# Shorter windows for the cached sequences, and the sampled rows' pass placed between the prompt's last units

## The reference, cut to what matters

```python
def finish(x, attn, pool, w_o, ...):
    mix = einsum(concat([attn, pool]), w_o)
    x1 = layer_norm(ALPHA * x + mix, ln1_g, ln1_b)
    hid = silu(x1 @ w_gate) * (x1 @ w_up)
    return layer_norm(ALPHA * x1 + hid @ w_down, ln2_g, ln2_b)

# prompt: q, k, v, logf, u = project(xp); attention over 1024 rows; pool_mix; finish
# sample, for each of 8 rows, with its own pages of the cache:
s = einsum(q, concat(cache_k[pages], k_new)) * 64 ** -0.5 + decay   # 8 heads, 4097 keys
out = einsum(softmax(s), concat(cache_v[pages], v_new))
# then finish() for the 8 rows, with the same weights (1024 x 2816 gate and up, 2816 x 1024 down)
```

## Time and profile before

| | us |
|---|---|
| median of 3 runs (1572.34 to 1581.2) | 1578.72 |
| profiled execution, own time | 1583.57 |
| its span, first to last instruction | 1581.6 |
| PE busy | 1397.7 (88%) |
| DVE busy | 719.6 (46%) |
| POOL busy | 551.9 (35%) |
| mean granted TensorE clock | 0.930 of full speed |

### The profile page before, as it was taken

How to read it: one execution, slowest core, us unless ns; L and a number is a source line. 1 busy time by engine, 2 the same in 40 slices (tenths; PEclk the granted TensorE clock), 3 DMA queues, 4 the chain that set the end, 5 groups by cost and what they waited for, 6 DMA issues and landing times.

```text
span 1581.6 us, 21048 instructions
## 1 busy us (share of the span) xinstructions
PE 1397.7 (88%) x7585; PEld 1110.2 (70%) x7585; DVE 719.6 (46%) x1000; ACT 361.4 (23%) x513; POOL 551.9 (35%) x211
## 2 busy tenths in 40 slices
PE   7998989999568458997999999999899999998875
PEld 5898989898468456775767767776677777766421
DVE  4745343445323283455444474635454634124702
ACT  4434444423100043211020112121102111111300
POOL 1010000031142335646555547375554572120500
PEclk9999999999778778998999999999999999999865
DMA  6321110100532304765667656686567665424895
GB/s 239 104 67 54 41 54 27 41 34 1 187 119 99 135 1 153 258 217 167 205 206 231 212 185 211 214 262 191 188 210 231 212 205 183 128 90 162 300 355 194
DMA packets 103031, 251.85 MB, mean 159 GB/s; under 512 B 12560, under 2 KB 13969, under 8 KB 97672
## 3 DMA queue, kind: packets, MB, share of 16 engines
q1 hardware_dynamic: 99632, 239.64, 45.5%
q0 software_dynamic: 3296, 10.88, 2.0%
HBM read 240.84 MB, written 9.86 MB: 159 GB/s over the span
## 4 chain that ended last, share of the span: by engine, by line
PE 73%; DVE 10%; DMA 7%; issue 3%; ACT 3%; SPq 3%; POOL 1%; DVEq 0%; ACTq 0%
PE PSM L1156 28%; PE PSM L1174 14%; PE PSM L959 10%; DMA AR<-ws 4%; PE PSM L1025 4%; PE PSM L1200 4%; PE PSM L1126 3%; PE PSM L972 3%; PE PSM L1011 2%; DMA WR<-w_o 1%; SPq L406 1%; SPq L401 1%; PE PSM L1271 1%; PE PSM L1258 1%; DVE PND L1609 1%
## 5 line engine op out<-in xcount | busy, mean ns | idle before, releaser
L627 POOL TENSOR_TENSOR AR<-AR,QB 128x2048 f32<-128x2048 f32 x64 | 298.6, 4671 | 162.7 <-DMA AR<-cache_k 162.5
L634 POOL TENSOR_TENSOR WL<-WR,WH 128x1024 fp32r<-128x1024 f32 x55 | 134.9, 2454 | 327.1 <-ACT WH L839 327.1
L1156 PE MATMUL PSM<-XH,WH 128*128 128x512 f32 x704 | 226.8, 403 | 0.0
L1156 PE MATMUL PSM<-XL,WH 128*128 128x512 f32 x704 | 221.9, 396 | 0.0
L1156 PE MATMUL PSM<-XH,WL 128*128 128x512 f32 x704 | 221.7, 396 | 0.0
L1531 DVE TENSOR_REDUCE SC<-AR 128x32 f32<-128x2048 f32 x64 | 145.8, 2278 | 101.8 <-POOL AR L627 101.8
L1646 DVE TENSOR_TENSOR ACC<-ACC,PSM 128x512 f32<-128x512 f32 x176 | 118.4, 684 | 136.4 <-PE PSM L1174 136.1
L1156 PEld LDWEIGHTS PSM<-XH,WH 128*128 128x128 f32 x704 | 129.0, 189 | 51.2 <-issue 23.5
L839 ACT CAST WH<-WR 128x1024 fp32r<-128x1024 f32 x55 | 57.6, 1048 | 469.3 <-PE PSM L1156 220.4
L1156 PEld LDWEIGHTS PSM<-XH,WL 128*128 128x128 f32 x704 | 133.1, 189 | 31.6
L1156 PEld LDWEIGHTS PSM<-XL,WH 128*128 128x128 f32 x704 | 133.0, 189 | 31.5
(11 more groups left out here) (233 smaller groups left out, 2121.6 us busy)
## 6 DMA issues: line engine op xcount, KB each, us to landing
AR<-cache_k SPq DMA_DIRECT2D x256, 256.0 KB, 3.3
AR<-cache_v SPq DMA_DIRECT2D x256, 256.0 KB, 3.4
AR<-ws SPq DMA_DIRECT2D x37, 1024.0 KB, 7.2
WR<-ffn SPq DMA_DIRECT2D x66, 512.0 KB, 4.6
WR<-w_in SPq DMA_DIRECT2D x16, 512.0 KB, 4.1
WR<-xT SPq DMA_DIRECT2D x8, 512.0 KB, 5.4
AR<-negF_d SPq DMA_DIRECT2D x8, 512.0 KB, 4.0
WR<-w_o SPq DMA_DIRECT2D x4, 1024.0 KB, 7.0
```

The source lines that it names most:

```text
L627: pool.tensor_tensor(keys, keys, QB[:].rearrange("p (o n) -> p o n", o=1).to_broadcast([P, CH, AW]), ALU.mult).then_inc(k_mul, 1)
L634: pool.tensor_tensor(lo, WR[:, e % WS, :], hi.bitcast(F32), ALU.subtract).then_inc(ffn_lo, 1)
L1156: ins = pe.matmul(out[:, hc], (hi, lo)[a][:, k * P:(k + 1) * P], x[b][:, k, hc], start=(k == 0 and n == 0), stop=(k == KC - 1 and n == 2))
```

## The change

The window of a cached sequence has 52 units instead of 62, so the 8 windows end at unit 416 and no longer at 496. The tables of units inside a window are drawn closer: the multiplications of keys stand 4 to 6 units apart and no longer 6 or 7, the values 11 or 12 units apart and no longer 15. The gap from the last values of a window to the first steps of the next stays as it was.

The sampled rows' pass is placed from unit 416 on. Its output product stands at 418 to 424, its first layer norm at 427 to 434, and the gate, up and down tiles at 438 to 521, some 2.5 units apart, so that all of it lies among the prompt's units. To free banks 0 and 1, which the prompt uses until its end, gate and up now share bank 7: a tile holds two chunks of gate and two of up, gate goes to column groups 0 and 1, up to 2 and 3. A full group has four such tiles GU, in place of two G and two U. One copy on ACT replaces the two copies of L895 and L1723, and the sum is made of four matmuls with a mask of 16 columns in place of eight with 8. The second layer norm of the 8 rows stands at units 523 to 525 of DVE's list. The layer norms' vectors g and b pass through one buffer, with a load between them (FACTORS1, OFFSETS1).

```diff
-WIN = 62
+WIN = 52
-VALUES = (9, 24, 39, 54)
+VALUES = (9, 21, 32, 44)
-OWN, COLUMNS, MAXIMUM, KEEP, HEADMAX = 57, 59, 60, 60, 61
-KMUL = (3, 10, 16, 23, 29, 36, 42, 49)
+OWN, COLUMNS, MAXIMUM, KEEP, HEADMAX = 47, 49, 50, 50, 51
+KMUL = (3, 8, 14, 19, 25, 30, 36, 40)
 KRED = tuple(o + 4 for o in KMUL)
 KLOAD = (0, 1) + tuple(o + 1 for o in KRED[:-2])
...
-        order += [(kind, g, r) for kind in "GU" for r in range(parts(g))]
-        order += [("D", g - 1, r) for r in range(parts(g - 1))] if g >= 1 else []
-        order += [("S", g, 0)]
...
+        order += [("GU", g, r) for r in range(parts("GU", g))]
+        order += [("D", g - 1, r) for r in range(parts("D", g - 1))] if g >= 1 else []
+    order += [("D", TGROUPS - 1, r) for r in range(parts("D", TGROUPS - 1))]
+    units = {step: TSTART + 5 * n // 2 + 3 * (n >= parts("GU", 0)) for n, step in enumerate(order)}
+    return units, [units["GU", g, parts("GU", g) - 1] + 2 for g in range(TGROUPS)]
...
-                if kind in "GU":
+                if kind == "GU":
...
-                            pe.wait_ge(silu_done, FT)
...
-                    rounds = ((r, 0),) if cols == HALF else ((0, 0), (1, 4 * cols))
-                    for k, at in rounds:
+                    elif r == 0:
+                        pe.wait_ge(e_hid, g)
+                    rounds, last = (1, 3) if cols == HALF else (2, 1)
+                    for a in range(rounds):
                         for q in range(4):
-                            ins = pe.matmul(PSM[32 * q:32 * q + 32, "GU".index(kind), 0:cols], CSP[:, 4 * k + q, :],
+                            k = 2 * (rounds * r + a) + q % 2
+                            ins = pe.matmul(PSM[32 * q:32 * q + 32, 7, 0:cols], CSP[:, k, :],
...
-                for kind, src in enumerate((gate_s, up_s)):
-                    for i in range(tiles):
-                        at = (4 * kind + i) * NB
-                        ins = pe.matmul(PSM[:, 7, at:at + NB], src[:, i * P:(i + 1) * P], blkmask[:], start=True, stop=True)
+                for i in range(min(4, FT - 4 * g)):
+                    ins = pe.matmul(PSM[:, 7, 2 * NB * i:2 * NB * (i + 1)], gu_s[:, i * P:(i + 1) * P], gumask[:],
+                                    start=True, stop=True)
...
-                dve.tensor_copy(up_s[:, 0:n], PSM[:, 1, 0:n]).then_inc(e_us, 1)
...
-            dve.wait_ge(t_used, len(STREAM))
-            sample_mean(2, e_var)
-            sample_scale(2)
+                if u == SAMPLE2:
+                    dve.wait_ge(t_used, len(STREAM))
+                    sample_mean(2, e_var)
+                if u == SAMPLE2 + 2:
+                    sample_scale(2)
```

More of the change, by code:

```diff
@@ L128, in sample_steps, with parts @@
 def sample_steps():
-    def parts(g):
-        return 2 if 4 * g + 4 <= FT else 1
     order = []
     for g in range(TGROUPS):
-        order += [(kind, g, r) for kind in "GU" for r in range(parts(g))]
-        order += [("D", g - 1, r) for r in range(parts(g - 1))] if g >= 1 else []
-        order += [("S", g, 0)]
[L138 to L144, removed]
+        order += [("GU", g, r) for r in range(parts("GU", g))]
[3 more added lines that the diff above has]
+    return units, [units["GU", g, parts("GU", g) - 1] + 2 for g in range(TGROUPS)]
+def parts(kind, g):
+    full = 4 * g + 4 <= FT
+    return {"GU": (2, 4), "D": (1, 2)}[kind][full]
+CSPAD = NB * WIN
+MIX, RESID, SQRT1, SCALE1, FACTORS1, OFFSETS1 = (CSPAD + n for n in (2, 11, 12, 13, 14, 18))
+TURN1, TURNED1, TSTART = (CSPAD + n for n in (20, 21, 22))
+STEPS_S, SUMS = sample_steps()
+STREAM = [("W", n, 0) for n in range(4)] + list(STEPS_S)
 TINDEX = {step: n for n, step in enumerate(STREAM)}
-SUNIT = {("W", n, 0): MIX + n for n in range(4)} | STEPS_S
+SUNIT = {("W", n, 0): MIX + 2 * n for n in range(4)} | STEPS_S
 NORM2 = BEGIN["D", NPAIR - 1] + 2
-LAST = max(SUNIT.values()) + 3
+SAMPLE2 = max(SUNIT.values()) + 2
+LNVEC2 = BEGIN["D", NPAIR - 1] - 4
+LAST = max(SAMPLE2 + 5, NORM2 + 2 * RT + 4)
 def weight_order():
@@ L886, in sample_root, with sample_partials @@
                 act.activation(sd[0:NB, RT, 0:1], sd[0:NB, RT, 1:2], ACT.Sqrt).then_inc(e_sd, 1)
-            def sample_gate(g):
+            def sample_partials(g):
                 n = min(HALF, DFF - g * HALF)
-                act.wait_ge(t_used, TINDEX["G", g, 0 if n < HALF else 1] + 1)
+                act.wait_ge(t_used, TINDEX["GU", g, parts("GU", g) - 1] + 1)
                 if g == 0:
-                    act.wait_ge(hl_done, FT)
+                    act.wait_ge(k_mul, NB * NCH)
                 else:
                     act.wait_ge(e_sum, g)
-                act.copy(gate_s[:, 0:n], PSM[:, 0, 0:n]).then_inc(e_gs, 1)
+                act.copy(gu_s[:, 0:n], PSM[:, 7, 0:n]).then_inc(e_gs, 1)
             def sample_silu(g):
@@ L903, in sample_silu @@
                     act.wait_ge(e_hid, g)
-                act.activation(hsilu[:, 0:tiles, :], PSM[:, 7, 0:tiles * NB].rearrange("p (a b) -> p a b", b=NB), ACT.Silu
-                               ).then_inc(e_silu, 1)
+                sums = PSM[:, 7, 0:2 * NB * tiles].rearrange("p (a b) -> p a b", b=2 * NB)
+                act.activation(hsilu[:, 0:tiles, :], sums[:, :, 0:NB], ACT.Silu).then_inc(e_silu, 1)
             for u in range(LAST):
@@ L1729, in sample_product @@
                     dve.wait_ge(t_used, TINDEX["D", g - 2, 1] + 1)
[L1730 to L1731 removed]
+                sums = PSM[:, 7, 0:2 * NB * tiles].rearrange("p (a b) -> p a b", b=2 * NB)
+                dve.tensor_tensor(hidp[:, g % 2, 0:tiles, 0:NB], hsilu[:, 0:tiles, :], sums[:, :, NB:], ALU.mult
                                   ).then_inc(e_hid, 1)
@@ L1821 @@
             blkmask[32 * j + h, h] = 1
+    gumask = np.zeros((P, 2 * NB), np.float32)
+    for j in range(4):
+        for b in range(NB):
+            gumask[32 * j + b, NB * (j // 2) + b] = 1
     cum = ((row[:, None] // NPAGE == row[None, :] // NPAGE) & (row[:, None] >= row[None, :])).astype(np.float32)
```

115 lines of the change are left out of this document (54 added, 61 removed).

## The result

| | before | after |
|---|---|---|
| median of 4 runs each, same chip, us | 1577.01 (1572.34 to 1581.2) | 1607.86 (1606.15 to 1610.84) |
| profiled span, us | 1581.6 | 1604.3 |
| mean granted TensorE clock | 0.930 | 0.938 |

The changed kernel is slower: the ratio is 1.0198, with a 95% interval of 1.0164 to 1.0233. The prediction said 1560 us in a range of 1538 to 1588, so both its side and its range were wrong.

The account below looks back on a forecast made before the run. Feed-forward part bound by TensorE, end by the sampled rows' weight stream; start of last group D 1448.35 + 36.3 + 10 - 3 + 9 + 4 = 1504.7, plus 58.5 gives span 1563.2, median 1560 us, range 1538 to 1588.

Parts of the forecast that it names:

- first unit: Start of the prompt's first unit: taken to stay at 606.4 us, as before.
- windows: Cached sequences: late key cycles on DVE reach TensorE by 1 to 2 us in each of 7 windows, +9 us.
- tiles, sums, output product, waits in the pass: Sampled rows' pass among the prompt's units on TensorE: +36.3 tiles, +10 sums, -3 output product, +4 waits.
- last group D to the end: Stretch to the program's end, DVE the busier engine: last store after 56 us, then 2.5, so 58.5 (55 to 64).
- Both fit on average: 52-unit windows: DMA at some 265 GB/s against 357 seen, and POOL busy some 43 of 50 us, both fit.
- signs of being wrong: Profile after: TensorE waiting for columns or additions, denominator's wait over 40 us, 0.63 us matmuls behind sums, end over 64.
- 16.4 us cycle: Seventh window before: one key buffer's round of reduction, load, multiplication, reduction, from 1243.41 to 1259.79.
- 24.1 us cycle: Seventh window before: another key-buffer round, 1251.57 to 1275.68, much of it put down to POOL waiting for the casting unit.
- Nearly all is hidden: Rival: windows bring -8, sums cost 1.3 each, no waits in the pass; 1536 to 1548 us, chance 0.17.
- The key cycle becomes the bound: Rival at DVE's reductions in all 7 windows: cycles of mean 20.3 us make the kernel slower, 1603 us; chance 0.08.
- The port at every window start: Rival: DVE's small copies wait for POOL's multiplications on the shared port at all 7 starts, 1591 us; chance 0.05.
- The pass disturbs the prompt: Rival: each sum keeps its wait and low clock (+15.5), or tiles come late; 1576 us, chance 0.12.

Follow-up runs that it names:

- e1: The kernel before with only the tables of the 52-unit windows, the sampled rows' pass as before: 1638.06 us, ratio 1.0404 to before.
- e3: The changed kernel with page numbers as constants, so SyncE loads none before a page's DMA: 1535.47 us, ratio 0.9733 to before.
- e5: The changed kernel with the value pages' number loads and DMA issues moved from SyncE's list to ScalarE's: 1547.18 us, ratio 0.9821 to before.
- e7: The changed kernel with the sampled rows' second layer norm moved behind the prompt's last row block: 1603.98 us, ratio 1.0179 to before.
- e8: The changed kernel with value pages issued by ScalarE and the sampled rows' second norm last: 1533.21 us, ratio 0.9738 to before.

## Why the prediction was wrong

Against the predicted span of 1563.2 us stand 1604.3, so 41.1 more. By the prediction's terms:

| term | predicted | measured | difference |
|---|---|---|---|
| first unit | 606.4, as before | 601.2 | -5 |
| windows | +9 | +58 (111 less 53) | +49 |
| tiles, sums, output product, waits in the pass | +47.3 | +36 | -11 |
| last group D to the end | 58.5 | 67.0 | +8.5 |

The first unit's 5 us are not the change's: e1, whose code up to there is before's, has it at 600.5.

**The windows.** This is the step that failed: "Both fit on average" weighed the DMA engines' rate and POOL's busy time, and then only the key cycle, with +9 for it. SyncE was in none of these sums, and its instructions are counted as busy in none of the rows that I read. The windows cost 58 us and not 9. Two of the prediction's signs of being wrong were there: TensorE waited for the columns and for additions (14.5 and 19.8 us), and the end was over 64 us. The trace of the kernel before already had what was needed. One line's records in the kernel after (count, and ns min/median/max) show it, and before's are alike:

```profile
L409 SPq TENSOR_LOAD <-page_sb x512: 260/266/487, 421.6 to 1324.4; - x171
L409 SPq FUSED_REGOPS  x512: 147/150/177, 422.1 to 1324.7; - x171
...
L414 SPq DMA_DIRECT2D AR<-cache_k x256: 332/333/1226, 424.6 to 1244.5; - x128
```

16 chunks at 4.3 us are 69 us of a sequence's 97 before, and 69 of 83 after: an in-order list that is 83% full by its own work, with waits for DVE, TensorE and POOL in it. That it fits on average says little, because what waits in it holds up everything behind. The 16.4 us cycle of the earlier trace rows already held it: from the reduction's end at 1243.41 to the load at 1246.47 SyncE was at work on the last value page and on four number loads. The 24.1 us cycle did not: its load was issued at 1251.75, 0.2 us after the reduction, and POOL's multiplication then waited in POOL's list until 1268.74, as the prediction says of it. I cannot say from the trace of before alone that 94 us would come out, but the room in the list was there to be counted.
**The rivals.** "Nearly all is hidden" fell with the forecast, in the same windows. "The key cycle becomes the bound" named the place and nearly the size: TensorE waited for additions and columns, and its 1603 us is within 5 of the measured 1607.86. It had a chance of 0.08, because I set the cycle's lengthening down to POOL's wait for the casting unit. The size was luck, the middle of two cycles seen before, and its cause was another one: e3 and e5 leave DVE's and POOL's part of that cycle as it was, and the kernel is fast. "The port at every window start" was wrong: the denominator's waits fell to 4.8 us. "The pass disturbs the prompt" was wrong too, by these rows of TensorE in the kernel after:

```profile
1489.62 0.96 PE L1287 MATMUL PSM<-gumask_sb,QB 128*128 128x16 f32 x8
1490.43 0.71 PE L1169 MATMUL PSM<-XH,WH 128*128 128x512 f32 x2
...
1491.99 1.06 PE L1278 MATMUL PSM<-AR,SC 128*32 128x512 f32 x8
...
1495.99 1.06 PE L1278 MATMUL PSM<-AR,SC 128*32 128x512 f32 x8
```

A sum takes 0.8 us, as do three others of the five (one took 0.9 behind a wait of 0.2), and the matmuls behind it run at full clock, where 2.0 had been put down; the granted clock is 1.00 from 1353 to 1537 us. Two tiles with two gate units between them are 4.00 us apart, so a tile costs 4.00 - 2.82 = 1.2. No tile of gate and up came late. These terms, 36 us in place of 47.3, were right in kind and a little too dear.

**The end** took 67.0 us where 58.5 was predicted, in a range of 55 to 64. Here the kernel after:

```profile
1537.29 0.47 PE L1187 MATMUL PSM<-WH,R 128*128 128x512 f32 x1 [3.81 <-DVE R L1638]
...
1567.53 2.78 DVE L1699 SCALAR_TENSOR_TENSOR AR<-AR,PSM 8x512 f32<-8x512 f32 x4
...
1570.34 1.27 DVE L1538 BATCH_NORM_STATS2 st<-AR 8x6 f32<-8x512 f32 x2
...
1572.80 0.79 PE L1187 MATMUL PSM<-WH,R 128*128 128x512 f32 x1 [3.47 <-DVE ACC L1647]
...
1599.59 0.57 POOL L675 DMA_DIRECT2D y_p<-ACC  x1 [0.30 <-POOL ACC L673]
```

And the prompt's last store in e7, whose last group D starts at 1538.99:

```profile
1591.53 0.57 POOL L675 DMA_DIRECT2D y_p<-ACC  x1 [0.30 <-POOL ACC L673]
```

The 8 rows' norm stands ahead of three of the prompt's row blocks, and TensorE's last unit waits 3.47 us for an addition queued behind it. The prompt's last store is issued 62.3 us after the group's start, where 56 was predicted, and 52.5 with the norm moved behind it in e7, close to the 50.9 of before. So the norm's place costs 9.8 us: the prediction let 3 of 8.3 be hidden, and nothing was. (e7 gains only 6.6 of them, because the norm then ends the program.) From that store to the span's end it takes 4.7 us where 2.5 was put down, a figure that no row had shown. These two make up most of the 8.5 us.

## What to carry to other kernels

Before a schedule is drawn closer, count the work of every list in it, also that of the engine that only issues: the number of register loads and issues times their spacing, against the new period. Then look for a closed round through such a list: if it waits for an engine which itself waits for something further down the same list, that round sets the pace and every rate "on average" is beside the point. Two independent streams of loads, each behind its own waits, belong in two lists; here that alone turned a loss of 2% into a gain of 1.8% (e5), and with the norm last into one of 2.6% (e8).

## What the runs showed of the hardware that was not expected

- A page number read into a register costs SyncE as much as the issue of the load that uses it: 0.55 and 0.52 us each. On ScalarE's list an issue itself took as long as on SyncE's, 0.34 us at the median against 0.33.
- An issue with a constant address took 0.43 us at the median (0.33 to 1.63), and 0.48 from one to the next against 0.52 with a register: little but the number's load is saved (e3).
- A streamed tile, with its four column groups, cost 1.2 us in the middle of full-array matmuls, 1.06 of it in its own matmuls, and the granted clock stayed at 1.00.
- Left open: how few units a window may have once the values have a list of their own, whether the weight loads and the values both taken off SyncE's list would bring more than e8 (not tried), and why a doubled number load costs before 129 us and not less.
